# First-layer projections as seven half-size products, before and behind the dilated attention

## The chip, the cores and the metric

The kernel runs on one core of one Trainium2 chip. The metric is the device time of one execution in microseconds (us), as the median of several runs.

## What is computed

The reference is a network of two blocks in float32. Only the front of the first block matters here. An input of 1024 tokens by 1024 features is multiplied by one weight matrix, whose columns give the operands of a dilated attention (8 heads of 64), of a gated scan (4 heads), two rank-16 gate inputs and an output gate:

```
proj = jnp.einsum('bsd,df->bsf', h, w_in).astype(jnp.float32)
qa, ka, va, qb, kb, vb, lr_f, lr_b, gate = _split(
    proj, (A_WIDTH, A_WIDTH, A_WIDTH, B_K_WIDTH, B_K_WIDTH, B_V_WIDTH, B_GATE_RANK, B_GATE_RANK, MIX_WIDTH))
oa = dilated_attention(heads(qa, A_HEADS), heads(ka, A_HEADS), heads(va, A_HEADS), rel_bias)
...
ob = bidirectional_gated_scan(qh, kh, heads(g_f, B_HEADS), kh, heads(g_b, B_HEADS), heads(vb, B_HEADS))
```

Widths: qa, ka, va 512 each, qb and kb 512 each, vb 1024, the two low-rank inputs 32 together. The second block needs a conditioning vector for each of two inputs, silu(c) times a matrix of 1024 by 6144; it does not depend on the first block.

## The kernel before

The program is a row of stages, each a block of its own with a barrier behind it. The tiles have 128 partitions. The input is turned once into `xT` (feature blocks by tokens; KB is 8 blocks of 128 features) and stays in SBUF. The stages that matter:

- **prologue** loads the input and the first two weight units, turns the input on PE into `xT`.
- **project** ("in0") makes qa, ka and va. A unit is 256 weight columns. For a CHANNEL unit (result is channels by tokens) the stationary operand is a weight block of 128x128 and the moving one 512 tokens of `xT`: 32 products of 512 columns (L227). For a TOKEN unit the stationary operand is a token tile of `xT` and the moving one 256 weight columns: 64 products of 256 columns (L233). A product (one matmul of the program) is two records in the trace, since float32 is passed twice. Weights are double-buffered, eight PSUM banks are drained by ACT and DVE in turns, and ACT issues the stores.
- **dilated_attention** ("att") has 96 slots: 4 pairs of heads times 24 slots (3 dilations of 8 query tiles). In slot g PE does turn(g) (the transposes of the probabilities, L1804), score(g+2) (L1793), values(g-1) (L1816), sometimes total(u) (L1824), and then a share of the projections for the next stage, `Background` (L391, L395): the low-rank columns, qb, kb and vb. DVE does bias(g) (L1854, L1858: scores plus bias table and the row maximum), three conditioning products weigh (L1866, L1868: weights `w_ada` times silu(c), summed into `acc`), and move_out(g-2) (L1874: the attention's result out of PSUM). ACT does exps(g) (L1899), move(g-1) (L1908) and the drain of the background's fills (L408). score(g+2) on PE waits for bias(g+1) on DVE. A slot is wide (256 keys) in the first two dilations and narrow (128 keys) in the third.
- A fill is one PSUM bank's worth of background work. Six fills run as a lead ahead of the first score; the rest is spread over the 96 slots by columns: the product that would be the n-th column of all goes to slot n*96/total. A fill that ends in slot e is drained in slot e+1, its store is issued at step e+2 of the SP loop. Three PSUM banks and three stage buffers go round.
- The conditioning weights come in 24 units of 1 MB in three buffers. Units 0 to 7 are weighed for both vectors (16 products, 5.3 slots), units 8 to 23 for one (8 products, 2.7 slots). The load of unit u+3 is issued once unit u has been weighed; total(u) sums over partitions on PE, and unit u+2 can't be begun before it.
- All loads and stores of the stage are issued by SP from one list, in program order: first weights, then (after POOL has set constants, `consts`) the inputs of the first two head pairs (load(0), load(1): 20 DMAs each), the conditioning weights, and then slot by slot. load(2) and load(3) are issued when the stage of the head pair two before is done.
- **low_rank_scan** ("gla") follows, with the output gate's projections behind it.

Of the kernel before, what the change touches and what calls it, by code (L numbers as in the profile page):

```python
# [51 lines left out]
def prologue(nc, tag, src, dst, rel_bias, buckets, vectors, vpad, c, c_ctx, sT, weights, wbuf):  # L52

    T = SEQ // P
    W = wbuf[0].shape[2]
    with ExitStack() as ctx:
# [18 lines left out]
        def _(sp):  # L75
            for t in range(T):
                sp.dma_start(raw[:, t, :], src[t * P:(t + 1) * P, :]).then_inc(raw_loaded[t], 16)
            for b in range(2):
                sp.dma_start(wbuf[b][:, :, :], weights.rearrange("(k p) n -> p k n", p=P)[:, :, b * W:(b + 1) * W]).then_inc(w_loaded, 16)
# [6 lines left out]
            sp.wait_ge(w_loaded, 32)  # L86
# [199 lines left out]
class Background:  # L286
# [113 lines left out]
    def move(self, act, g):  # L400

        for f, end in enumerate(self.ended_in):
            if end != g - 1:
                continue
            job, m = self.job_of(f), self.count(f) // KB * self.columns(f)
            act.wait_ge(self.filled, f + 1)
            wait(act, self.stored[f % self.stages], 16 * (f // self.stages))
            act.activation(self.stage[f % self.stages][0:job.rows, 0:m], self.ps[f % self.banks][0:job.rows, 0:m], ACT.Copy).then_inc(self.moved, 1)  # L408

# [1199 lines left out]
def dilated_attention(nc, tag, qT, kT, vpad, vectors, attn, jobs, sT, ada_w, ada):  # L1609
# [6 lines left out]
    LEAD = 6  # L1616
# [3 lines left out]
    with ExitStack() as ctx:  # L1620
# [9 lines left out]
        p_sb = sb("p_sb", [P, 2, 2, 256])  # L1630
# [11 lines left out]
        w_ada = sb("w_ada", [P, 3, KB, ADA_W])  # L1642
        acc, ones, row = sb("acc", [P, 2, 2, ADA_W]), sb("ones", [P, 1]), sb("row", [1, 2, 2, ADA_W])
        ps_a = pbank("ps_a")
        ada_loaded, ada_stored = [sem(f"ada_loaded{b}") for b in range(3)], [sem("ada_stored0"), sem("ada_stored1")]
        weighted, summed, row_moved = (sem(n) for n in ("weighted", "summed", "row_moved"))
        bg = Background(sb, sem, pbank, jobs, HEADS * ST, 3, 3, 3, lead=LEAD)
# [46 lines left out]
        def _(sp):  # L1694
# [31 lines left out]
            def load_ada(u):  # L1726
                wait(sp, weighted, u - 2)
                src = ada_w[:, u * ADA_W:(u + 1) * ADA_W].rearrange("(k p) n -> p k n", p=P)
                sp.dma_start(w_ada[:, u % 3, :, :], src).then_inc(ada_loaded[u % 3], 16)

            def store_ada(u):
                sp.wait_ge(row_moved, u + 1)
                n = rows_of(u)
                sp.dma_start(ada[0:n, u * ADA_W:(u + 1) * ADA_W].rearrange("(a r) c -> a r c", a=1), row[:, u % 2, 0:n, :]).then_inc(ada_stored[u % 2], 16)
# [10 lines left out]
            bg.begin(sp)  # L1745
# [3 lines left out]
            load_ada(0)  # L1749
            load_ada(1)  # L1750
            load_ada(2)
            for g in range(LEAD):
                bg.transfer(sp, g)
            for g in range(HEADS * ST):
                bg.transfer(sp, LEAD + g)
                if g + 1 in unit_due and unit_due[g + 1] + 3 < ADA_UNITS:
                    load_ada(unit_due[g + 1] + 3)
                if g - 3 in unit_due:
                    store_ada(unit_due[g - 3])
# [5 lines left out]
            for b in range(2):  # L1765
                sp.wait_ge(ada_stored[b], 8 * ADA_UNITS)
# [4 lines left out]
        def _(pool):  # L1771
            make_identity(pool, ident)
# [7 lines left out]
            pool.memset(ident[0:1, 0:1], 1.0).then_inc(consts, 1)  # L1780

        @block.tensor
        def _(pe):
# [13 lines left out]
            def turn(g):  # L1797
# [4 lines left out]
                for h in range(2):  # L1802
                    for c in range(wide(d) // P):
                        last = pe.transpose(ps_t[:, h * 256 + c * P:h * 256 + (c + 1) * P], p_sb[:, s % 2, h, c * P:(c + 1) * P], ident[:, :])  # L1804
# [21 lines left out]
            pe.wait_ge(consts, 1)  # L1826
            for g in range(LEAD):
                bg.multiply(pe, g)
            score(0)
# [13 lines left out]
        def _(dve):  # L1843
            def bias(g):
# [6 lines left out]
                wait(dve, p_done, g - 1)  # L1851
# [8 lines left out]
            def weigh(u, kb, r):  # L1860
                if kb == 0 and r == 0:
                    dve.wait_ge(ada_loaded[u % 3], 16 * (u // 3 + 1))
                    wait(dve, summed, u - 1)
                mine, w, s = acc[:, u % 2, r, :], w_ada[:, u % 3, kb, :], sT[:, kb, r:r + 1]
# [11 lines left out]
            dve.wait_ge(consts, 1)  # L1876
            for g in range(HEADS * ST):
# [7 lines left out]
                if g > 1:  # L1885
                    move_out(g - 2)
            move_out(HEADS * ST - 2)
# [3 lines left out]
        def _(act):  # L1891
            def exps(g):
# [3 lines left out]

                wait(act, p_turned, g - 1)
# [3057 lines left out]
```

## Time and profile before

| | us |
|---|---|
| median of three runs | 4059.78 |
| the three runs | 4050.93 to 4068.09 |
| profiled execution, its run time | 4055.85 |
| profiled execution, span of the trace | 4054.2 |
| mean granted TensorE clock, share of full speed | 0.927 |

The trace is of one execution, with times from its start. In it the prologue lasts to 25.7 us, the projections ("in0") from 25.7 to 192.9 us, the attention stage from 199.0 to 689.3 us; of these its 96 slots from 260.1 to 683 us. PE is TensorE's matmul, PEld its weight load (it overlaps PE), DVE VectorE, ACT ScalarE, POOL GpSimd, SP SyncE; "SPq" is SP issuing a DMA. In a timeline the first two columns are start and duration, and brackets hold the idle time before the group and what ended it.

### The profile page before, as it was taken

How to read it: one execution, taken by the hardware profiler on the slowest of the kernel's cores; microseconds unless marked ns; L12 is line 12 of the kernel's file. 1: busy time of each engine (PE TensorE's matmuls, PEld its weight loads, DVE VectorE, ACT ScalarE, POOL GpSimd, SP SyncE). 2: the span in 40 equal slices, each digit the busy share in tenths (PEclk: the TensorE clock that was granted, in tenths of full speed). 3: DMA queues.
4: the chain of work that ended last, by engine and by line, in shares of the span. 5: the costliest groups of instructions: out<-in, count | busy, mean ns of one | idle time of the engine just before them, and what ended most of it. 6: DMA issues, size and time to landing. Idle time of an engine off the chain costs nothing. (4 is left out here: it accounts for less than half of the span.)

```text
span 4054.2 us, 47003 instructions
## 1 busy us (share of the span) xinstructions
PE 3560.9 (88%) x16369; PEld 2321.4 (57%) x16369; DVE 1821.6 (45%) x4038; ACT 1081.7 (27%) x2206; POOL 1179.5 (29%) x948
## 2 busy tenths in 40 slices
PE   8989998999798999999987698998877776949996
PEld 4645676777344667567546347564556775524442
DVE  1025552443573456666665460323479476240011
ACT  1023333442342233332432450221213212101111
POOL 0000000343343455555564362001212444211110
PEclk9999998999899999999999896998987877969998
DMA  3264542231532111211212532123334722347996
GB/s 116 68 183 143 151 133 86 80 103 58 217 147 60 55 57 45 66 56 41 72 38 71 220 137 76 47 64 101 105 86 144 252 75 101 121 185 241 319 320 233
DMA packets 409824, 494.01 MB, mean 122 GB/s; under 512 B 70514, under 2 KB 314506, under 8 KB 409603
## 3 DMA queue, kind: packets, MB, share of 16 engines
q1 hardware_dynamic: 380983, 457.42, 34.0%
q0 software_dynamic: 4608, 16.78, 1.6%
q10 hardware_dynamic: 24012, 16.97, 1.3%
q8 instruction: 126, 2.06, 0.2%
q14 instruction: 95, 0.78, 0.1%
HBM read 362.32 MB, written 128.77 MB: 121 GB/s over the span
## 5 line engine op out<-in xcount | busy, mean ns | idle before, releaser
L821 POOL TENSOR_TENSOR hgrn_queries<-hgrn_qd,hgrn_pair_decay 128x640 f32<-128x640 f32 x192 | 279.4, 1475 | 290.5 <-PE hgrn_ps_a L936 255.6
L871 PE MATMUL hgrn_ps_w<-xT,hgrn_ring 128*128 128x512 f32 x432 | 195.8, 600 | 1.8 <-PEq L34 1.8
L395 PE MATMUL gla_bg_ps<-gla_bg_w,xT 128*128 128x256 f32 x768 | 186.6, 388 | 4.3 <-DMA gla_bg_w<-in_w_in_ab_dram 4.3
L1473 PE MATMUL end_ps_z<-end_w,end_yT 128*128 128x512 f32 x384 | 168.7, 600 | 1.8 <-DMA end_w<-in_w_out_ab_dram 1.1
L2577 PE MATMUL end_ps_z<-end_w,end_yT 128*128 128x512 f32 x384 | 168.4, 599 | 0.8 <-ACT end_yT L2505 0.8
L395 PEld LDWEIGHTS gla_bg_ps<-gla_bg_w,xT 128*128 128x128 f32 x768 | 145.1, 194 | 35.0 <-issue 10.6
L391 PE MATMUL att_bg_ps<-xT,att_bg_w 128*128 128x512 f32 (+1 forms) x288 | 136.6, 614 | 13.3 <-POOL att_ident L1780 13.3
L45 POOL MEMSET gla_ident<- 128x128 f32 x1 | 0.2, 204 | 483.3 <-POOLq L34 483.3
L871 PEld LDWEIGHTS hgrn_ps_w<-xT,hgrn_ring 128*128 128x128 f32 x432 | 81.7, 193 | 94.1 <-issue 93.9
L871 PE MATMUL hgrn_ps_w<-hgrn_xs,hgrn_wsum 128*128 128x512 f32 x288 | 129.8, 599 | 5.3 <-ACT hgrn_sig L1153 5.3
L1041 DVE TENSOR_TENSOR hgrn_k_end<-hgrn_kd,hgrn_end_decay 128x128 f32<-128x128 f32 x168 | 127.1, 796 | 9.2 <-issue 2.6
L876 PE MATMUL hgrn_ps_w<-hgrn_ring,xT 128*128 128x256 f32 x576 | 128.8, 380 | 0.0
L2933 PE MATMUL in_ps<-hT_cols,in_w 128*128 128x512 f32 x288 | 126.2, 593 | 0.0
L1473 PEld LDWEIGHTS end_ps_z<-end_w,end_yT 128*128 128x128 f32 x384 | 73.1, 192 | 92.5 <-issue 89.0
L2577 PEld LDWEIGHTS end_ps_z<-end_w,end_yT 128*128 128x128 f32 x384 | 73.3, 193 | 90.5 <-issue 89.3
L4793 PE MATMUL exp_ps_d<-expw_wd,exp_hidT 128*128 128x512 f32 x256 | 114.2, 599 | 11.0 <-ACT exp_hidT L4740 11.0
L395 PE MATMUL att_bg_ps<-att_bg_w,xT 128*128 128x256 f32 x512 | 123.4, 387 | 0.0
L1899 ACT ACTIVATE att_p_sb<-att_s_sb,att_shift 128x256 f32<-128x256 f32 (+1 forms) x192 | 88.8, 464 | 121.4 <-DVE att_shift L1858 121.3
L227 PE MATMUL in_ps<-xT,in_wbuf 128*128 128x512 f32 x256 | 111.9, 600 | 9.0 <-PEq L34 9.0
L876 PEld LDWEIGHTS hgrn_ps_w<-hgrn_ring,xT 128*128 128x128 f32 x576 | 108.2, 191 | 14.1 <-issue 0.5
L4775 PE MATMUL exp_ps_g<-expw_wg,exp_xT 128*128 128x512 f32 x256 | 115.2, 604 | 0.7 <-ACT exp_xT L4729 0.7
L1056 DVE COPY_PREDICATED hgrn_scores<-hgrn_mask,hgrn_ps_s 128x128 f32<-128x128 uint32 x192 | 48.9, 299 | 147.2 <-issue 147.2
(645 smaller groups left out, 7744.2 us busy)
## 6 DMA issues: line engine op xcount, KB each, us to landing
expw_wg<-in_exp_w_gate_dram SPq DMA_DIRECT2D x16, 2048.0 KB, 10.3
expw_wu<-in_exp_w_up_dram SPq DMA_DIRECT2D x16, 2048.0 KB, 16.3
expw_wd<-in_exp_w_down_dram SPq DMA_DIRECT2D x16, 2048.0 KB, 21.9
att_w_ada<-in_ada_w_dram SPq DMA_DIRECT2D x24, 1024.0 KB, 6.3
hgrn_ring<-in_w_in_c_dram SPq DMA_DIRECT2D x18, 1024.0 KB, 5.4
end_gt<-gate_l SPq DMA_DIRECT2D x16, 768.0 KB, 8.5
hgrn_ring<-in_w_in_c_dram SPq DMA_DIRECT2D x24, 512.0 KB, 5.5
hgrn_o<-hgrn_o_stage SPq DMA_DIRECT2D x192, 64.0 KB, 1.6
```

The lines of the kernel that those rows point to most:

```text
L227: last = pe.matmul(bank[0:job.rows, 0:job.span], w[:, k, b * job.rows:(b + 1) * job.rows], job.acts[:, k, s:s + job.span], start=(k == 0), ...
L391: last = pe.matmul(bank[0:job.rows, 0:job.span], w[:, k, b * job.rows:(b + 1) * job.rows], job.acts[:, k, s:s + job.span], start=(k == 0), ...
L395: last = pe.matmul(bank[0:job.rows, q * job.width:(q + 1) * job.width], job.acts[:, k, t * P:t * P + job.rows], w[:, k, 0:job.width], star ...
L821: pool.tensor_tensor(queries[:, d, s, :].rearrange("p (b a c) -> p b a c", b=POINTS, a=PC), q, f, ALU.mult).then_inc(queries_done, 1)
L871: last = pe.matmul(bank[:, :], a[:, k, :], x(k), start=(fresh and k == 0), stop=(k == HK - 1), skip_group_check=True)
L876: last = pe.matmul(bank[:, q * 2 * P:(q + 1) * 2 * P], x(k)[:, t * P:(t + 1) * P], a[:, k, :], start=(fresh and q == 0 and k == 0), stop=( ...
L1041: dve.tensor_tensor(k_end[:, d, p % 2, :].rearrange("p (a c) -> p a c", c=CH), kd[:, b, d, t * P:(t + 1) * P].rearrange("p (a c) -> p a c" ...
L1473: made = pe.matmul(ps_z[h][:, :], yT[:, k, :], w[:, k, h * BANK:(h + 1) * BANK], start=(k == 0), stop=(k == NB - 1))
L2577: made = pe.matmul(ps_z[h][:, :], yT[:, k, :], w[:, k, halves[h]], start=(k == 0), stop=(k == NB - 1))
L2933: last = pe.matmul(ps[(3 * n + part) % 2][:, 0:span], w[u % 3][:, k, b * P:(b + 1) * P], acts, start=(k == 0), stop=(k == KB - 1))
L4775: last = pe.matmul(ps_g[:, :], xT[:, b, k, :], wg[:, b, k, :], start=(k == 0), stop=(k == KB - 1))
L4793: last = pe.matmul(ps_d[g][:, :], hidT[:, j, :], wd[:, b, j, g * BANK:(g + 1) * BANK], start=(j == 0), stop=(j == FB - 1))
```

## The change

Every projection of the first layer up to vb is computed in Strassen's form (Winograd's variant): the input `xT` and each weight unit of 256 columns are cut in two halves in both of their dimensions, and seven products of half the depth and half the width take the place of eight. Four sums of the input are made once (class `Halves` takes them as `xs`, and one quarter of `xT` is changed in place and restored at the start of low_rank_scan); four sums of each weight unit are made on POOL (`sums`, into `wsum` and into the unit itself). The seven products of a unit are seven fills: three of them are snapshots that ACT copies from PSUM to a stage buffer (`move`), three are added to such a snapshot by DVE on the way out (`join`), and the last is copied by ACT. A CHANNEL fill is 4 products of 512 columns, a TOKEN fill 16 products of 128 columns.

- `project` gives way to `project_halves`: first the low-rank columns (16 products of 512 columns, before in the attention's lead), then 6 units (qa, ka, va), one fill per step, SP issuing the stores. It ends by loading the first two units of the attention's background.
- In the attention, `Background` gives way to `Halves` with 8 units (56 fills) and 12 leading fills in place of 6 (34 fills before). PE no longer waits for `consts` before the lead, but before the first score. POOL makes the first unit's sums ahead of the constants. DVE joins at the end of its slot, behind move_out.
- Three stage buffers have fixed roles in place of going round: the fill LAST of unit u is moved into the buffer from which fill JOIN22 of the same unit has been stored.
- The conditioning weights have two buffers in place of three (load(u+2) when u has been weighed) and the row one in place of two; the probabilities are written over the scores, and bias(g) waits for turn(g-2) in place of exps(g-2).
- The prologue also loads the low-rank columns (128 KB).

The core of the diff:

```diff
-            dilated_attention(nc, "att", qa, ka, vpad, vectors, attn, [
-                Job(CHANNEL, xT, SEQ, w, 5 * A + B, 2 * RANK, 1, low),
-                Job(CHANNEL, xT, SEQ, w, 3 * A, 256, 2, qb),
-                Job(CHANNEL, xT, SEQ, w, 4 * A, 256, 2, kb),
-                Job(TOKEN, xT, SEQ, w, 5 * A, 256, 4, vb),
-            ], sT, ada_w_2[0], ada)
+            first = channels(0, qa) + channels(A, ka) + tokens(2 * A, vpad[VPAD:VPAD + SEQ, :], A)
+            second = channels(3 * A, qb) + channels(4 * A, kb) + tokens(5 * A, vb, B)
...
+                    project_halves(nc, "in0", xT, xs, ring, wsum, stage, first, second[0:2], low_w, low)
+                dilated_attention(nc, "att", qa, ka, vpad, vectors, attn, xT, xs, ring, wsum, stage, second, sT, ada_w_2[0], ada)
```

The roles of the seven fills, their banks and stage places, and what moves and joins wait for:

```diff
+    ROLE = {SNAP1: 0, PLAIN: 1, SNAP21: 0, SNAP22: 2, JOIN22: 0, JOIN21: 2, LAST: 0}
+    PLACE = {SNAP1: 0, PLAIN: 0, LAST: 2, SNAP21: 1, JOIN21: 1, SNAP22: 2, JOIN22: 2}
...
+    def move(self, act, g):
...
+            act.wait_ge(self.filled, f + 1)
+            wait(act, self.stored[place], 16 * {SNAP22: 2 * u, LAST: 2 * u + 1}.get(i, u))
+            act.activation(self.stage[:, place, :], self.ps[self.bank_of[f]][:, :], ACT.Copy).then_inc(self.moved, 1)
+
+    def join(self, dve, g):
...
+            dve.wait_ge(self.filled, f + 1)
+            dve.wait_ge(self.moved, self.nth[snap])
+            dve.tensor_tensor(into, self.ps[self.bank_of[f]][:, :], into, ALU.add).then_inc(self.added, 1)
...
+    def multiply(self, pe, g, x_made=None):
...
+                e = self.before_on[f]
+                if e is not None:
+                    pe.wait_ge(self.added if self.fills[e][1] in self.BY_DVE else self.moved, self.nth[e])
```

`before_on[f]` is the fill that used the same bank before. With three banks in the attention, bank (u + role) mod 3, fill SNAP21 of a unit waits for SNAP1 of that unit to be moved.

```diff
             def load_ada(u):
-                wait(sp, weighted, u - 2)
+                wait(sp, weighted, u - 1)
...
-            bg.begin(sp)
+            bg.load(sp, 2)
+            load_ada(0)
             sp.wait_ge(consts, 1)
             load(0)
             load(1)
-            load_ada(0)
             load_ada(1)
-            load_ada(2)
             for g in range(LEAD):
                 bg.transfer(sp, g)
             for g in range(HEADS * ST):
                 bg.transfer(sp, LEAD + g)
-                if g + 1 in unit_due and unit_due[g + 1] + 3 < ADA_UNITS:
-                    load_ada(unit_due[g + 1] + 3)
+                if g + 1 in unit_due and unit_due[g + 1] + 2 < ADA_UNITS:
+                    load_ada(unit_due[g + 1] + 2)
...
-                wait(dve, p_done, g - 1)
+                wait(dve, p_turned, g - 1)
...
                 if g > 1:
                     move_out(g - 2)
+                bg.join(dve, LEAD + g)
...
+            low_rows = slice(0, KB // 2)
+            dve.tensor_tensor(xT[:, low_rows, BANK:SEQ], xT[:, low_rows, BANK:SEQ], xT[:, low_rows, 0:BANK], ALU.add).then_inc(restored, 1)
```

Three places show the moved instructions. The first is SP's queue at the start of the attention stage, before the change: the loads of the second head pair end (the last `att_tab`), three conditioning loads follow, and then the first stores of the lead's fills.

```order
L1711 DMA att_tab<-vectors 128x128
L1729 DMA att_w_ada<-in_ada_w_dram 128x8x256 x3
L347 DMA low<-att_bg_stage 32x512
L336 DMA att_bg_w<-in_w_in_ab_dram 128x8x256
L347 DMA low<-att_bg_stage 32x512
L347 DMA qb<-att_bg_stage 128x512 x3
```

The same place after it.

```order
L1956 DMA att_tab<-vectors 128x128
L1974 DMA att_w_ada<-in_ada_w_dram 128x8x256
L508 DMA qb<-l_stage 128x512 x3
L489 DMA l_ring<-in_w_in_ab_dram 128x8x256
L508 DMA qb<-l_stage 128x512 x4
L489 DMA l_ring<-in_w_in_ab_dram 128x8x256
```

The first stores of fills still stand behind all loads of two head pairs; one conditioning load went ahead of them and one is gone.

The second place is DVE in a slot of the attention, before: after move_out comes the next slot's bias.

```order
L1874 COPY att_stage<-att_ps_o 128x128
L1854 ISA att_s_sb,att_stage<-att_ps_s,att_tab 128x256
L1854 ISA att_stage 128x1
L1854 ISA att_s_sb,att_stage<-att_ps_s,att_tab 128x256
L1854 ISA att_stage 128x1
L1858 TENSOR_SCALAR att_shift<-att_stage 128x2
```

After, in a slot that follows the end of a joined fill.

```order
L2120 COPY att_stage<-att_ps_o 128x128
L588 TENSOR_TENSOR l_stage<-att_bg_ps,l_stage 128x512
L2100 ISA att_s_sb,att_stage<-att_ps_s,att_tab 128x256
L2100 ISA att_stage 128x1
L2100 ISA att_s_sb,att_stage<-att_ps_s,att_tab 128x256
L2100 ISA att_stage 128x1
L2104 TENSOR_SCALAR att_shift<-att_stage 128x2
```

The join came between move_out and the next bias; there are 20 of them behind the slots and 4 in the lead.

The third place is SP's queue behind the load of the fourth head pair (load(3)), before.

```order
L1711 DMA att_tab<-vectors 128x192 x4
L1711 DMA att_tab<-vectors 128x128
L1729 DMA att_w_ada<-in_ada_w_dram 128x8x256
L1734 DMA ada<-att_row 1x256
L351 DMA vb<-att_bg_stage 128x2x256
L1729 DMA att_w_ada<-in_ada_w_dram 128x8x256
```

After.

```order
L1956 DMA att_tab<-vectors 128x192 x4
L1956 DMA att_tab<-vectors 128x128
L489 DMA l_ring<-in_w_in_ab_dram 128x8x256
L1974 DMA att_w_ada<-in_ada_w_dram 128x8x256
L1979 DMA ada<-att_row 1x256
L508 DMA vb<-l_stage 128x4x128
L1974 DMA att_w_ada<-in_ada_w_dram 128x8x256
```

The first conditioning load behind load(3) was that of unit 13 and is now that of unit 12, and a weight load of 1 MB stands ahead of it.

## Rows read from the trace of the kernel before

**Rows 1.** Busy time by stretch, inside the attention: PE, PEld, DVE, ACT, POOL, clock, DMA.

```profile
300.00:350.00 50.00, 50.00 (x215) 28.72 (x215) 25.26 (x100) 18.37 (x60) 0.00 (x0) 1.00 0.33 101
```

**Rows 2.** The first projections' two product lines, and their first sixteen records.

```profile
L227 PE MATMUL in_ps<-xT,in_wbuf x256: 592/592/1192, 25.7 to 137.0; 128*128 128x512 f32 x128
...
L233 PE MATMUL in_ps<-in_wbuf,xT x256: 378/379/380, 137.4 to 192.5; 128*128 128x256 f32 x128
...
25.68 8.90 PE L227 MATMUL in_ps<-xT,in_wbuf 128*128 128x512 f32 x16 [9.04 <-PEq L34]
```

**Rows 3.** PE in order of time, products of 128 columns in the second layer.

```profile
1402.85 0.39 PE L933 MATMUL hgrn_ps_a<-hgrn_v_in,hgrn_scores 128*128 128x128 f32 x2
...
1403.74 7.07 PE L876 MATMUL hgrn_ps_w<-hgrn_ring,xT 128*128 128x256 f32 x32
```

**Rows 4.** SP's queue in order of time, from the attention stage's start.

```profile
199.02 1.65 SPq L336 DMA_DIRECT2D att_bg_w<-in_w_in_ab_dram  x3
206.12 0.34 SPq L1698 DMA_DIRECT2D att_q<-qa  x1
...
239.32 5.88 SPq L1729 DMA_DIRECT2D att_w_ada<-in_ada_w_dram  x3
245.25 2.83 SPq L347 DMA_DIRECT2D low<-att_bg_stage  x1
```

**Rows 5.** ACT behind the lead; landing of the load issued at 239.3.

```profile
254.15 0.60 ACT L408 ACTIVATE att_bg_stage<-att_bg_ps 128x512 f32<-128x512 f32 x1 [24.38 <-DMA low<-att_bg_stage]
...
257.66 1.28 ACT L1899 ACT_TABLE_LOAD   x1
...
DMA to landing us min/median/max: 8.6/8.6/8.6
```

**Rows 6.** PE at the attention stage's start, in order of time.

```profile
206.15 43.58 PE L391 MATMUL att_bg_ps<-xT,att_bg_w 128*32 128x512 f32 x96 [13.31 <-POOL att_ident L1780]
249.66 0.70 PE L1793 MATMUL att_ps_s<-att_k,att_q 64*128 64x256 f32 x4
...
260.10 1.12 PE L1804 MATMUL att_ps_t<-att_ident,att_p_sb 128*128 128x128 f32 x4 [7.75 <-ACT att_p_sb L1899]
```

**Rows 7.** All engines around one slot of the attention.

```profile
325.07 1.94 PE L391 MATMUL att_bg_ps<-xT,att_bg_w 128*128 128x512 f32 x4
325.27 0.29 DVE L1874 COPY att_stage<-att_ps_o 128x128 f32<-128x128 f32 x1 [3.65 <-PE att_ps_o L1816]
325.48 0.41 DVE L1854 CUSTOM_DVE_ANT_0 att_s_sb<-att_ps_s,att_tab 128x256 f32<-128x256 f32 x1
...
326.32 0.17 DVE L1858 TENSOR_SCALAR att_shift<-att_stage 128x2 f32<-128x2 f32 x1
...
326.84 0.60 PE L1804 MATMUL att_ps_t<-att_ident,att_p_sb 128*128 128x128 f32 x4
...
327.37 0.84 PE L1793 MATMUL att_ps_s<-att_k,att_q 64*128 64x128 f32 x4
```

**Rows 8.** Second layer: a join on DVE, a weight sum on POOL, DVE beside POOL.

```profile
L970 DVE TENSOR_TENSOR hgrn_gstage<-hgrn_ps_w,hgrn_gstage x20: 677/692/693, 1315.3 to 1928.7; 128x512 f32<-128x512 f32 x20
...
L762 POOL TENSOR_TENSOR hgrn_wsum<-hgrn_ring x24: 1261/1272/2437, 1240.8 to 2113.3; 128x512 f32<-128x512 f32 x18, 128x1024 f32<-128x1024 f32 x6
...
L1041 DVE TENSOR_TENSOR hgrn_k_end<-hgrn_kd,hgrn_end_decay x168: 277/750/2439, 1367.8 to 2202.0; 128x128 f32<-128x128 f32 x168
```

**Rows 9.** SP around the fourth head pair's load; landing of the load at 494.27.

```profile
474.94 0.62 SPq L1724 DMA_DIRECT2D attn<-att_stage  x1
...
492.89 0.43 SPq L1729 DMA_DIRECT2D att_w_ada<-in_ada_w_dram  x1
...
DMA to landing us min/median/max: 11.9/11.9/11.9
```

**Rows 10.** DVE begins conditioning unit 12.

```profile
492.50 0.35 DVE L1866 TENSOR_SCALAR att_acc<-att_w_ada,sT 128x256 f32<-128x256 f32 x1 [3.12 <-PE att_ps_a L1824]
```

**Rows 11.** Who waited for whom in the slots: total, times, longest.

```profile
DVE att_acc L1866 <- PE att_ps_a L1824: 46.1, 15, 4.3
```

More of the change, by code:

```diff
@@ L1771, in _ @@
         def _(pool):
+            bg.sums(pool, 0)
             make_identity(pool, ident)
@@ L1780, in _ @@
             pool.memset(ident[0:1, 0:1], 1.0).then_inc(consts, 1)
+            for u in range(1, len(units)):
+                bg.sums(pool, u)
         @block.tensor
@@ L1876, in _ @@
             dve.wait_ge(consts, 1)
+            for g in range(LEAD):
+                bg.join(dve, g)
             for g in range(HEADS * ST):
@@ L4831, in network @@
             w = w_in_ab[0]
-            with ExitStack() as first_weights:
-                wbuf = [first_weights.enter_context(nc.sbuf_tensor(f"in0_wbuf{b}", [P, KB, 256], F32)) for b in range(2)]
-                prologue(nc, "pro", x[0], xT, rel_bias, buckets, vectors, vpad, c_2, c_ctx_2, sT, w, wbuf)
-                project(nc, "in0", [
-                    Job(CHANNEL, xT, SEQ, w, 0, 256, 2, qa),
-                    Job(CHANNEL, xT, SEQ, w, A, 256, 2, ka),
-                    Job(TOKEN, xT, SEQ, w, 2 * A, 256, 2, vpad[VPAD:VPAD + SEQ, :]),
-                ], loaded=wbuf)
@@ L4840, in network @@
[L4840 to L4847 removed]
+            low_at = 5 * A + B
@@ new lines, in network @@
+            channels = lambda col, dst: [Unit(CHANNEL, w, col + UNIT_W * n, dst, UNIT_W * n) for n in range(A // UNIT_W)]
+            tokens = lambda col, dst, width: [Unit(TOKEN, w, col + UNIT_W * n, dst, UNIT_W * n) for n in range(width // UNIT_W)]
+            first = channels(0, qa) + channels(A, ka) + tokens(2 * A, vpad[VPAD:VPAD + SEQ, :], A)
+            second = channels(3 * A, qb) + channels(4 * A, kb) + tokens(5 * A, vb, B)
+            with ExitStack() as shared:
+                held = lambda n, *shape: shared.enter_context(nc.sbuf_tensor(n, [P, *shape], F32))
+                ring, wsum = held("l0_ring", 3, KB, UNIT_W), held("l0_wsum", 3, KB // 2, P)
+                stage, xs = held("l0_stage", 3, BANK), held("l0_xs", 3, KB // 2, BANK)
+                with nc.sbuf_tensor("l0_low_w", [P, KB, 2 * RANK], F32) as low_w:
+                    prologue(nc, "pro", x[0], xT, rel_bias, buckets, vectors, vpad, c_2, c_ctx_2, sT, w, ring, low_w, low_at)
+                    project_halves(nc, "in0", xT, xs, ring, wsum, stage, first, second[0:2], low_w, low)
+                dilated_attention(nc, "att", qa, ka, vpad, vectors, attn, xT, xs, ring, wsum, stage, second, sT, ada_w_2[0], ada)
@@ L4848, in network @@
+            low_rank_scan(nc, "gla", 4, B // 4, qb, kb, vb, low, gla_gate_up[0], gla_gate_bias[0], gla_o, 1 / 16, scale, xT, [
+                Job(TOKEN, xT, SEQ, w, low_at + 2 * RANK, 256, 6, gate_l0),
             ])
```

246 lines of the change are left out of this document (217 added, 29 removed).

## The prediction

> **What bounds the kernel now.** I read the stretches first, then each engine's timeline over three places. Inside the attention PE is busy for the whole 50 us at the full clock (1.00), while DVE has 25 us of work and ACT 18 [rows 1]. So in the slots each product taken off PE shortens the time, as long as DVE, ACT and SP keep up. Two places differ. At the stage's start SP spends 206.1 to 239.3 us issuing the loads of two head pairs, and only at 245.25 comes the first store of a fill [rows 4]; ACT stands until 254.15 on that store, and PE, which finished the lead at 249.7, can turn only at 260.1 [rows 5, 6]. The second is SP around load(3): 18 us from 474.9 to 492.9 pass before a conditioning load gets through [rows 9].
>
> **Price of a product.** 128 products of 512 columns run from 25.68 to 137.4; the first sixteen records take 8.9 us, the other 120 products 103 us, 0.858 each. The start at the half clock (1.2 GHz) costs 1.9 us more. 128 products of 256 columns take from 137.4 to 192.7, 0.432 each [rows 2]. The nearest thing to the new TOKEN products is four pairs of records of 128 columns, each with its own weight load, between 1402.85 and 1403.74: 0.111 a record, 0.223 a product [rows 3]. A CHANNEL unit so falls from 32 to 28 products of 0.858 (27.5 to 24.0 us), a TOKEN unit from 64 x 0.432 = 27.6 to 112 x 0.223 = 25.0 us.
>
> The Trainium skill, "TensorE: Matmul & The Clock Gate", section "Back-to-back issue gap", speaks against this step: in a stream of weight loads and products it gives about 81 ns a matmul at 128 columns where the isolated gap is 56. No run here shows that ratio; the row above stands at the bare column rate.
>
> **The change, part by part** (against the profiled execution, 4055.85 us; it lies 3.9 us under the median and inside the spread of the three runs).
>
> *Projections ahead of the attention.* Four CHANNEL units give 16 x 0.858 = 13.7 us, two TOKEN units 55.3 - 50.0 = 5.3, and the low-rank products (16, one pass of 512 columns each) come in from the lead: +13.7. Sum -5.3. The four input sums on DVE and the first weight sums on POOL lie beside those low-rank products. Later weight sums: three of 1.27 us and the gaps between them (4.3 us, rows 8) must be ready two fills (6.9 us) after the last unit's end: hidden, for as long as POOL does nothing else. The prologue's extra 128 KB in small lines: 0 to 2 us, I take +0.7. The last store is 256 KB in place of 1 MB, so the barrier comes sooner: 0 to -2, I take -1.
>
> *The lead.* Call the attention stage's start T (199.0). Before, the first turn is at T + 61.1 [rows 4, 6]. PE may now start at T, not at T + 7.1. But the stage buffers decide. POOL makes four sums first (4 x 1.43 = 5.7 us), so `consts` comes at T + 12.8, and load(0) and load(1) take 33.2 us of SP: T + 46.0. Only then, behind one conditioning load, come the stores. That load lands 8.6 us after its issue [rows 5], the two stores PLAIN and JOIN22 of unit 0 (0.5 MB) some 1.4 us later by the 2.8 us per MB at which the two further loads pushed the low-rank store back [rows 4, 5]: T + 56.0. LAST of unit 0 is moved into JOIN22's place, so ACT stands until then; behind it stands the move of SNAP1 of unit 1, and PE's tenth fill waits for that. PE has done nine fills (36 x 0.858 + 1.9 = 32.8 us), idles some 24 us, resumes at T + 57.4 at the half clock, does 12 products (10.3 + 1.9) and scores at T + 69.6. Bias and score take 1.9 us, table load, exponentials and turn 2.4 (257.66 to 260.10, rows 5, 6): turn at T + 74. Cost: **+13 us**. Bounds: 0 if small stores pass the load ahead of them and PE resumes 13 us sooner, +18 if SP is held at each store as before (2.8 us).
>
> *The slots: less PE work.* Before 96 products of 512 columns and 256 of 256, now 64 and 448 of 128: -27.5 - 10.7 = **-38.2 us**, 0.4 a slot.
>
> *The slots: joins on DVE.* The join sits behind move_out and ahead of the bias for which score waits. Before: values' issue ends at 325.07, DVE copies at 325.27, bias is done at 326.49, PE reaches score at 327.37, 0.53 after turn: 0.9 us of slack [rows 7]. After a joined fill ends (F), DVE starts 0.2 later, holds 0.60 for the join (0.69 long, rows 8, started on by 0.09), 1.01 for bias, 0.05 to PE: F + 1.86. PE wants it at the end of the slot's products plus 0.53. The stall is 1.33 less what PE still multiplies in that slot behind F. By the plan's rule, of 19 joined fills that end in slots seven end with the slot (9.3 us), three have one product of 512 columns behind them (0.47 each, 1.4), and nine TOKEN ones have two (three fills, 0.88), three (0.66), four (two fills, 0.44), five (0.22) or six (none): 4.4. Sum **+15 us**; bounds 5 (wait times partly absorbed) and 19 x 1.33 = 25. ACT's drains were there before, and its exponentials have a whole slot of slack.
>
> *The slots: conditioning in two buffers.* At one-row units a load has about three slots. It lands in 5 to 12 us [rows 5, 9]; while SP is free that is enough. Not at load(3): SP is held from 474.9 to 492.9, then issues 1 MB of weights and only then unit 12's load, which is thus the second megabyte, and the second one before (494.27) landed 11.9 us on, at 506 [rows 9]. DVE reached unit 12 at 492.5 [rows 10]; in slots 0.4 us shorter that is 491. It waits 14.5 us with the bias queued behind, PE stands with it, and restarts at the half clock: **+16.5 us**; bounds 6 and 20. Load(2) falls among two-row units with twice the time: 0.
>
> *Smaller terms.* DVE already waits 46 us in 15 units for total(u-2) [rows 11]; with 0.4 us less of products behind it PE feels more of that: 0 to 6, I take +3. POOL's 24 sums in the slots run beside DVE, and an instruction of DVE beside POOL had a median of 0.75 us where its least was 0.28 [rows 8]; this meets the weighs rather than the bias: 0 to 10, +3. The Trainium skill, "SBUF — State Buffer", section "SBUF: two separate sides", has the rule: a DVE instruction with two SBUF inputs and a GpSimd one exclude each other for the whole instruction. By it no weigh waits over 1.27 us, and bias and join, which read one operand from PSUM, don't wait. The shorter idle before the first turn saves a half-clock start: -1. Writing the probabilities over the scores costs nothing: turn(g-2) stands ahead of score(g) on PE, which bias(g) waits for anyway. Restoring `xT` is one DVE instruction of four times a join's columns, at a stage start where DVE has nothing: 0, at most 2.8.
>
> **Sum:** -5.3 + 0.7 - 1 + 13 - 38.2 + 15.1 + 16.5 + 3 + 3 - 1 = +5.8; 4055.85 + 5.8 = 4061.7, so **4062 us**. PE loses 43.5 us of work and gets it back as waiting.
>
> **Rivals.**
> 1. *The waits are mostly absorbed (faster).* PE's queue and DVE's idle half [rows 1] swallow them: lead +5 (small stores pass), joins +8, unit 12's load +6. That is 8 + 7 + 10.5 = 25.5 less: 4036. For it: DVE was idle 3.65 us ahead of the copy in rows 7. Against: what counts is the order behind it, and the idle time lies ahead of the copy. Chance 0.22.
> 2. *Two conditioning buffers are late at every one-row unit (slower).* Decisive is whether issue delay plus landing exceeds three slots, 12 us. A store that waits for a joined fill can hold SP most of a slot (4 us); with 5 to 7 us of landing it is short of 12, behind another megabyte it is over. If 13 more units are late by 2 us: +26, 4088. Chance 0.14.
> 3. *128-column products are held by their weight loads (slower).* At 1.45 times 0.223, 672 products cost 0.10 each more: +67, 4129. The ratio of the two figures of the skill's page on TensorE, above, is 1.45. For it: weight loads of 0.19 us each lie behind one another. Against: rows 3. Chance 0.06.
> 4. *The change doesn't do what it says:* fills blocked in banks and places throughout, beyond the lead. The roles leave two fills between a store and its reuse, about 7 us against a landing of 3: 0.03, some 4100.
>
> **How the numbers follow.** The forecast has 0.55; its terms' bounds (lead -13/+5, joins -10/+10, unit 12 -10/+4, small ones -6/+10) give 4040 to 4082. With rival 1 below and rival 2 above, 8 in 10 lie in **4034 to 4090**. Half a percent (20 us) is about what measuring this kernel can tell from no change. Faster by more (under 4039.5): rival 1 with most of its chance and the forecast's lower edge, 0.24. Slower by more (over 4080): rivals 2 to 4 and the upper edge, 0.20. Within: 0.56.
>
> **What would show it.** PE idle of some 24 us within the lead, ended by ACT's move of SNAP1, itself ended by a store of `qb`; the first turn 74 us behind the stage's start. A DVE wait of 10 to 15 us at the first `att_acc` of unit 12, ended by a DMA, and no like wait elsewhere. PE waits on `att_shift` of 0 to 1.3 us, some 19 of them with a join in front. Products of 128 columns 0.111 apart a record: were they 0.16, rival 3 holds. "in0" 5 us shorter. Wrong it would be if the first turn came by T + 62, or if the slots took under 405 us (423 before, 422 by my terms).

## The result, and the profile after

| | kernel before | changed kernel |
|---|---|---|
| median of the runs | 4057.65 us (4050.93 to 4068.09, 9 runs) | 4071.05 us (4066.08 to 4080.92, 9 runs) |
| ratio to before | 1 | 1.0034, interval 1.0023 to 1.0045 |
| profiled execution: own time | 4055.85 us | 4071.05 us |
| first projections ("in0"), first to last product | 167.2 us | 162.3 us |
| attention stage's start, T | 199.0 | 192.75 |
| first turn | T + 61.1 | T + 71.7 |
| first turn to last values | 423.1 us | 431.8 us |

The forecast was 4062 us with a range of 4034 to 4090, and no change as the likeliest case: 0.56. The time came inside the range, 9 us above the forecast and 0.34% above the kernel before.

PE in order of time over the start of the attention stage and at its end (start, length, what it does, in brackets the idle time before it and what ended it):

```profile
185.06 3.74 PE L562 MATMUL in_ps<-l_wsum,xT 128*128 128x128 f32 x32
192.79 9.62 PE L560 MATMUL att_bg_ps<-xT,l_ring 128*128 128x512 f32 x16 [4.00 <-PEq L34]
...
249.40 8.65 PE L560 MATMUL att_bg_ps<-l_xs,l_wsum 128*128 128x512 f32 x16 [22.95 <-ACT l_stage L576]
257.88 3.60 PE L560 MATMUL att_bg_ps<-xT,l_ring 128*128 128x512 f32 x8
261.40 0.70 PE L2039 MATMUL att_ps_s<-att_k,att_q 64*128 64x256 f32 x4
...
264.49 0.66 PE L2050 MATMUL att_ps_t<-att_ident,att_s_sb 128*128 128x128 f32 x4 [0.42 <-ACT att_s_sb L2147]
...
695.76 0.56 PE L2062 MATMUL att_ps_o<-att_v,att_pT 128*128 128x64 f32 x4
```

These rows answer to [rows 6]. PE starts the lead at the stage's first moment, does nine fills, stands 22.95 us and turns at 264.49. What it stood for is in ACT's and SP's timelines, answering to [rows 5] and [rows 4]:

```profile
248.26 1.08 ACT L576 ACTIVATE l_stage<-att_bg_ps 128x512 f32<-128x512 f32 x2 [38.34 <-DMA qb<-l_stage]
...
258.69 1.28 ACT L2147 ACT_TABLE_LOAD   x1
```

```profile
205.35 0.34 SPq L1943 DMA_DIRECT2D att_q<-qa  x1
...
219.15 1.17 SPq L1943 DMA_DIRECT2D att_q<-qa  x1
...
237.12 0.43 SPq L1974 DMA_DIRECT2D att_w_ada<-in_ada_w_dram  x1
237.61 3.95 SPq L508 DMA_DIRECT2D qb<-l_stage  x3
```

SP issues load(0) and load(1) from 205.35 to 237.1, then a conditioning load of 1 MB, and only then the stores of `l_stage`, one of which ACT needs: 38.34 us of standing on ACT, 22.95 of them felt by PE.

The second place is unit 12. SP's queue (answering to [rows 9]), then DVE (to [rows 10]) and PE:

```profile
474.24 0.66 SPq L1943 DMA_DIRECT2D att_q<-qa  x1
...
490.88 1.03 SPq L489 DMA_DIRECT2D l_ring<-in_w_in_ab_dram  x1
491.96 0.72 SPq L1974 DMA_DIRECT2D att_w_ada<-in_ada_w_dram  x1
```

```profile
503.12 0.35 DVE L2112 TENSOR_SCALAR att_acc<-att_w_ada,sT 128x256 f32<-128x256 f32 x1 [13.81 <-DMA att_w_ada<-in_ada_w_dram]
```

```profile
505.21 1.23 PE L2039 MATMUL att_ps_s<-att_k,att_q 64*128 64x256 f32 x4 [11.97 <-DVE att_shift L2104]
```

The waits over the whole stage, 190 to 700 us (engine, what it waited for; us in total, times, longest):

```profile
PE att_ps_s L2039 <- DVE att_shift L2104: 36.0, 28, 12.0
...
PE att_bg_ps L560 <- ACT l_stage L576: 22.9, 1, 22.9
...
DVE att_acc L2112 <- DMA att_w_ada<-in_ada_w_dram: 13.8, 1, 13.8
```

In the slots alone (264 to 697) the first row is 34.7 us in 27 waits; in the kernel before the same row, 262 to 683, is 0.8 us in two. Less the 12.0 of unit 12, that leaves 22.7 us in 26 short waits.

A third place lies behind the slots, at the start of low_rank_scan. PE's first product there waits for POOL to make `gla_ident`; the first row is from the kernel before, the others from the changed one:

```profile
693.78 0.69 PE L2142 MATMUL gla_ps_s<-gla_ident 128*128 128x128 f32 x2 [10.60 <-POOL gla_ident L2050]
...
702.80 2.29 DVE L2516 TENSOR_TENSOR xT<-xT 128x2048 f32<-128x2048 f32 x1 [6.15 <-PEq L34]
703.16 2.08 POOL L47 TENSOR_SCALAR_AFFINE_SELECT gla_ident<-gla_ident 128x128 f32<-128x128 f32 x1 [0.20 <-issue]
708.83 0.69 PE L2390 MATMUL gla_ps_s<-gla_ident 128*128 128x128 f32 x2 [12.51 <-POOL gla_ident L2298]
```

POOL's instruction, 0.29 us in the kernel before, takes 2.08 and ends 0.15 us behind DVE's restoring of `xT` (702.80 to 705.09). PE waits 12.51 us in place of 10.60.

What the prediction had far too small is in the stretches (busy time of the engines, then PE's granted clock, DMA share, GB/s), which answer to [rows 1]:

```profile
300.00:350.00 50.00, 47.35 (x207) 27.08 (x206) 26.66 (x98) 18.16 (x59) 0.00 (x0) 0.97 0.26 81
340.00:350.00 10.00, 8.77 (x30) 4.12 (x29) 5.28 (x21) 2.89 (x11) 0.00 (x0) 0.83 0.28 83
500.00:550.00 50.00, 42.21 (x264) 33.16 (x265) 24.82 (x85) 17.22 (x52) 0.00 (x0) 0.88 0.34 106
```

and the same at 500 in the kernel before:

```profile
500.00:550.00 50.00, 50.00 (x271) 37.86 (x269) 24.56 (x90) 18.46 (x57) 0.00 (x0) 1.00 0.50 162
```

Stretches of 10 us from 270 to 680 all have clock 1.00 in the kernel before. In the changed kernel twelve of those up to 690 have less: 0.83 to 0.86 at 340, 420, 550 and 570, 0.91, 0.50 and 0.91 from 490 to 520, and five between 0.90 and 0.99. Length times (1 - clock), added up, is 15.3 us. About 3.5 us of it falls where PE stood for unit 12 (493.2 to 505.2), which costs nothing twice; **12 us** is left: 3.3 behind unit 12's wait, and five dips of 1.7 us each (at 340, 410 to 430, 540 to 560, 570 to 590, 650 to 670). Most short waits have no dip behind them: 26 waits stand beside five dips, and two waits of 1.27 us (ending at 370.0 and 471.7) were followed by none. What decides it isn't shown by any run here. How such a dip looks in PE's own rows:

```profile
341.36 0.38 PE L2050 MATMUL att_ps_t<-att_ident,att_s_sb 128*128 128x128 f32 x2
342.97 0.84 PE L2039 MATMUL att_ps_s<-att_k,att_q 64*128 64x128 f32 x4 [1.23 <-DVE att_shift L2104]
343.75 0.66 PE L2062 MATMUL att_ps_o<-att_v,att_pT 128*128 128x64 f32 x4
344.33 1.60 PE L2070 MATMUL att_ps_a<-att_acc,att_ones 128*1 128x512 f32 x2
345.87 2.07 PE L560 MATMUL att_bg_ps<-xT,l_wsum 128*128 128x512 f32 x2
347.74 0.54 PE L2050 MATMUL att_ps_t<-att_ident,att_s_sb 128*128 128x128 f32 x2
...
349.47 1.94 PE L560 MATMUL att_bg_ps<-xT,l_wsum 128*128 128x512 f32 x4
```

After a wait of 1.23 us, two records of 512 columns take 1.60 and two more 2.07; four take 1.94 a slot later. In stretches of 1 us the granted clock is 0.82 from 344 to 345, 0.50 from 345 to 348 and 0.98 from 348 to 349: the half clock (1.2 GHz) comes some 1.7 us behind the wait's end, and the full one (2.4 GHz) is back some 5 us behind it.

### The profile page after: what moved, and what is told of

It reads as the page before. It is cut to its first block and busy times, and to the rows that moved or that the text cites. A ratio compares the mean times of both kernels' runs of the same rounds, so it can differ in the third digit from the quotient of the medians.

```text
span 4069.3 us, 48185 instructions
## 1 busy us (share of the span) xinstructions
PE 3533.5 (87%) x16881; PEld 2323.9 (57%) x16881; DVE 1866.2 (46%) x4073; ACT 1087.5 (27%) x2218; POOL 1252.8 (31%) x1004
## 5 line engine op out<-in xcount | busy, mean ns | idle before, releaser
L530 POOL TENSOR_TENSOR l_wsum<-l_ring 128x512 f32<-128x512 f32 x14 | 20.0, 1432 | 548.9 <-PE att_bg_ps L562 202.4
L2147 ACT ACTIVATE att_s_sb<-att_s_sb,att_shift 128x256 f32<-128x256 f32 (+1 forms) x192 | 88.9, 464 | 169.9 <-DVE att_shift L2104 169.8
L2114 DVE SCALAR_TENSOR_TENSOR att_acc<-att_w_ada,sT,att_acc 128x256 f32<-128x256 f32 x224 | 118.7, 543 | 14.2 <-issue 0.9
L2039 PE MATMUL att_ps_s<-att_k,att_q 64*128 64x256 f32 (+1 forms) x384 | 91.5, 559 | 36.1 <-DVE att_shift L2104 36.0
L2321 POOL TENSOR_TENSOR gla_queries<-gla_qd,gla_pair_decay 128x640 f32<-128x640 f32 x64 | 87.2, 1382 | 84.5 <-PE gla_ps_o L2384 61.0
```

The costliest lines, as they stand in the source:

```text
L2114: last = dve.scalar_tensor_tensor(out=mine, in0=w, scalar=s, in1=mine, op0=ALU.mult, op1=ALU.add)
```

## Experiments on the four waits

Where did 43 us of saved PE work go? My theory: into three separate waits (the lead, the joins, unit 12), each with lost clock behind it. The rival: they are one limit, DVE or SP, which shows up elsewhere once one of them is removed. Five kernels change one thing each. All ran against the same kernel before, whose median was 4056.87 to 4057.65 us in every group of runs; the ratios have intervals of 0.1 to 0.2% (4 to 6 us) either way, so two gains that lie closer than that can't be ranked.

**Head-pair loads in pieces.** SP no longer issues a load of 20 DMAs at once, but two a slot:

```
-                    load(j + 2)
+                if j and s < 10 and j + 1 < HEADS:
+                    load(j + 1, slice(2 * s, 2 * s + 2))
```

> The changed kernel, but the 20 DMAs of load(2) and of load(3) are issued two per slot over ten slots (24 to 33, 48 to 57) in place of in one piece. My theory: unit 12 of the conditioning is late only because SP is held 17 us by load(3). So DVE's 13.8 us wait at unit 12 falls to under 3 us, PE's 12.0 us wait at score goes with it, and so does the stretch at the half clock behind it (499 to 512 us in the changed kernel's trace, some 5 us lost): 12 + 5 = 17 us less, 4054. Rival (the load is late because two buffers are too few at one-row units, whoever holds SP): the wait moves to other one-row units, less than 5 us gained, over 4066.

Measured: 4052.57 us, 0.9991 of before (0.9982 to 1.0001), so 18.5 us less than the changed kernel. The longest wait of PE at score is 1.9 us, and DVE has no wait for `att_w_ada` any more. Unit 12's late load was SP's doing. In the changed kernel's own rows it costs 15.3 us, 12.0 of waiting and 3.3 of half clock behind it, where 16.5 had been put down; that the run gave 18.5, with load(2) spread as well, lies within the intervals.

**The lead's stores ahead of load(1).**

```
             load(0)
-            load(1)
...
                 bg.transfer(sp, LEAD + g)
+                if g < 10:
+                    load(1, slice(2 * g, 2 * g + 2))
```

> The changed kernel, but load(1) is no longer issued ahead of the lead's stores: its 20 DMAs go two per slot over slots 0 to 9. My theory: PE's 22.9 us wait in the lead is ACT's wait for the store of fill JOIN22, which stands behind load(1) and load(0) on SP. Without load(1) SP is free 17 us sooner, at 22 us behind consts' 12.6, and the store lands at about T + 36, when PE has just done its ninth fill (T + 33): the wait falls to 0 to 4 us, score comes at about T + 48 in place of T + 68.7, 20 us less, 4051. Rival (SP is only late, not the cause; the next loads in the slots are pushed back in turn): the first slots wait for stores and conditioning loads instead, less than 8 us gained, over 4063.

Measured: 4057.43 us, 0.9995 (0.9985 to 1.0005), 13.6 less. PE's wait in the lead fell, but not to the 0 to 4 us that I had expected:

```profile
PE att_bg_ps L560 <- ACT l_stage L576: 7.9, 1, 7.9
```

and the first turn came 15.4 us sooner. The slots then took 1.1 us more, with unit 12's wait at 13.6 and more half clock around it (0.52 and 0.63 in the 10 us stretches at 480 and 490). The remaining 7.9 us are, for the most part, the stores' landing behind the 1 MB conditioning load, which is still issued ahead of them: the last version below takes that load away too, and the wait falls to 1.0.

**The join behind the next slot's bias.** DVE still does every join, one slot later:

```
                 bias(g)
+                if g:
+                    bg.join(dve, LEAD + g - 1)
...
-                bg.join(dve, LEAD + g)
```

> The changed kernel, but DVE joins a fill one slot later and behind bias, not ahead of it; the joins and their number stay. My theory: 27 waits of PE at score in the slots, 22 us without the long one, come mostly from joins that stand ahead of the bias; with the half-clock stretches that follow some of them (344, 419, 549, 574 to 584, 659 us: 8 us lost by the granted clock) they cost 20 to 30. Expected: 15 to 22 us less, 4052, and PE's waits at score under 8 us beside unit 12's. Rival (the waits come from POOL's sums that stretch DVE's weighs, or from the total-before-weigh wait, which stay): under 6 us gained, over 4065.

Measured: 4051.49 us, 0.9985 (0.9976 to 0.9995), 19.6 less. PE's waits at score, 190 to 690:

```profile
PE att_ps_s L2039 <- DVE att_shift L2104: 23.5, 15, 12.4
```

The short waits, without unit 12's, fell from 24.0 to 11.1 us, 12.9 less (I had expected under 8 to be left). Most of the other 6.7 was clock: the stretches from 330 to 430 lose 1.7 us here and 3.4 in the changed kernel, those from 520 to 670 none, and 5.1 in the changed kernel; around unit 12 (480 to 520) it lost 1.8 more than there.

**Small joins.** Is it the join's work or its place?

```
-                bg.join(dve, LEAD + g)
+                bg.join(dve, LEAD + g, 8)
```

> The changed kernel, with each join in the attention's slots over 8 of its 512 columns (the rest of the sum is left out, so the projections made in the slots are incomplete); order, waits and stores are as before. It separates the join's 0.69 us of DVE work from its place: DVE standing on the fill's end with the bias queued behind. Theory: the place weighs as much as the work. By the prediction's own terms a stall of 1.33 us less what PE has behind the fill becomes one of 0.73: seven fills that end with the slot keep 0.73 (5.1 us) and the others about 1 in all, so 15 falls to 6, plus some clock: 9 to 13 us less, 4060. Rival: only the work counts; then taking it away is worth what moving it behind the bias was, 19.6: 4051.5.

Measured: 4058.94 us, 1.0000 (0.9989 to 1.0011): 12.1 less, by the first theory. Short waits are 16.8 us:

```profile
PE att_ps_s L2039 <- DVE att_shift L2104: 29.9, 23, 13.1
```

The same joins done in full behind the bias give more (19.6) than joins with hardly any work in their old place. The difference fits DVE standing on the fill's end with the bias queued behind; the two runs' intervals just overlap, so the order of the two is likely and not certain.

**Small weight sums on POOL.**

```
             for u in range(1, len(units)):
-                bg.sums(pool, u)
+                bg.sums(pool, u, few=True)
```

> The changed kernel, but POOL makes the weight sums of units 1 to 7 of the attention over 8 of 128 columns only; the rest of the sums is left out. Takes away POOL's 1.27 us instructions beside DVE and nothing else. My theory: each set of sums stretches one slot's weighs (three weighs of 1.44 us took 4.46 at 483 us), PE feels 0.5 to 1.5 us of it, six times: 3 to 9 us less, 4065. Rival (they are the main cause of the waits at score): 15 us less or more, under 4057.

Measured: 4063.89 us, 1.0014 (1.0005 to 1.0024), 7.2 less, short waits 18.8 us where the changed kernel has 24.0. Its trace is of an execution of 4072.82 us, 8.9 above that median, so the 5.2 us less of waits can't be set against the 7.2 one to one. In the changed kernel the trace shows how it comes about. POOL's four sums of one unit, and DVE beside them:

```profile
481.76 1.27 POOL L530 TENSOR_TENSOR l_wsum<-l_ring 128x512 f32<-128x512 f32 x1 [59.90 <-PE att_bg_ps L562]
...
486.05 1.27 POOL L536 TENSOR_TENSOR l_wsum<-l_ring,l_wsum 128x512 f32<-128x512 f32 x1 [0.16 <-issue]
```

```profile
482.42 0.63 DVE L2104 TENSOR_SCALAR att_shift<-att_stage 128x2 f32<-128x2 f32 x1
483.14 4.46 DVE L2114 SCALAR_TENSOR_TENSOR att_acc<-att_w_ada,sT,att_acc 128x256 f32<-128x256 f32 x3
...
505.25 1.60 DVE L2114 SCALAR_TENSOR_TENSOR att_acc<-att_w_ada,sT,att_acc 128x256 f32<-128x256 f32 x3
```

```profile
488.79 0.70 PE L2039 MATMUL att_ps_s<-att_k,att_q 64*128 64x256 f32 x4 [1.46 <-DVE att_shift L2104]
```

Three weighs took 4.46 us beside POOL and 1.60 without it, so about 0.95 more each; bias and PE behind them were late by 1.46. The Trainium skill's rule on the shared port ("SBUF — State Buffer", "SBUF: two separate sides"), cited in the prediction, agrees for the weighs: each was held back by no more than one sum's 1.27. That bias doesn't wait, which the prediction drew from the rule, holds in this trace for its two reductions (0.41 us each, as always) and not for its last instruction, which reads SBUF alone: L2104 took 0.63 us at 482.42 until the first sum ended, where its median is 0.17, and up to 1.26 elsewhere in the slots.

## Is it the waits that bring the clock down?

The changed kernel has two new things in its slots: waits of about a microsecond, and 448 projection products of 128 columns, each with a weight load of its own. Either could lie behind the dips. The kernel before has neither, and no dip. (The attention's own turns and narrow scores have 128 columns in both kernels, so "no 128-column products" in the expectations holds for the projections only.) So I gave it the waits alone, by doing DVE's two bias reductions, and the drain behind them, three times in 24 of 96 slots; in the first kernel every fourth, in the second in four groups of six:

```
-                for h in range(2):
+                for h in (0, 1, 0, 1, 0, 1) if 2 < g % 4 else range(2):
```

```
+                for h in (0, 1, 0, 1, 0, 1) if 11 < g % 24 < 18 else range(2):
```

> The kernel before (no 128-column products in its slots, no clock loss in them either), with DVE's two bias reductions done three times in every fourth slot (24 of 96), so that PE waits at score for DVE there. Four more reductions of 0.4 us are 1.6 us, less the 0.9 us of slack of rows 7: 0.7 us of PE wait in 24 slots, 17 us. Theory: the chip answers clusters of such short waits with a lower granted clock, so the slots lose 5 to 12 us more to the clock where they lost none: 4057 + 17 + 8 = 4082. Rival: the clock loss of the changed kernel comes from its 128-column products with their many weight loads, not from waits; then the granted clock in these slots stays 1.00 and the time is 4057 + 17 = 4074.

> As the kernel whose bias reductions are done three times in 24 slots of the kernel before, but with those slots in four groups of six on end (12 to 17 of every 24). The PE waits are the same 17 us. Theory: if it is waits that bring the clock down, then waits close together do it more surely than waits apart: the groups show a granted clock of 0.5 to 0.9 and lose 5 to 15 us more, 4057 + 17 + 10 = 4084, with the clock at 1.00 in the slots between the groups. Rival (128-column products are the cause): clock 1.00 throughout the slots, 4074.

Measured: 4078.67 us, 1.0053 (1.0037 to 1.0068), and 4074.64 us, 1.0045 (1.0029 to 1.0060): 21.2 and 17.2 us above the kernel before. PE's waits at score, slots apart and slots together:

```profile
PE att_ps_s L1793 <- DVE att_shift L1859: 13.0, 19, 0.9
```

```profile
PE att_ps_s L1793 <- DVE att_shift L1859: 10.2, 13, 1.2
```

and one stretch of each in which the clock fell:

```profile
330.00:340.00 10.00, 9.12 (x36) 5.57 (x37) 5.35 (x25) 3.57 (x13) 0.00 (x0) 0.83 0.73 234
```

```profile
420.00:430.00 10.00, 9.11 (x35) 4.87 (x34) 7.59 (x34) 2.48 (x8) 0.00 (x0) 0.83 0.01 3
```

| | waits more than before | clock lost, 270 to 680, before: 0 | sum | measured |
|---|---|---|---|---|
| waits apart | 12.2 | 6.8 | 19.0 | 21.2 |
| waits together | 9.4 | 8.5 | 17.9 | 17.2 |

The times alone would not decide, since the waits came out shorter than the 17 us I had put down. The clock does: it fell in five and in six stretches (four and five dips of 1.7 us) of slots whose projections have no product of 128 columns. Short waits are enough; over all of them, each microsecond of waiting lost another 0.6 to 0.9 to the clock. These are averages over a few dips in one execution each, and no price of a single wait: again most waits have no dip behind them. DVE's extra work by itself isn't the cause: in the first of the two stretches shown DVE was busy for 5.35 of 10 us, and the kernel before has 6.73 (600 to 610 us) at a clock of 1.00. The part of my expectation on groups held as to place (the dips at 310, 420 to 450 and 540 to 570 lie at three of the four groups), while the total over the groups is hardly above that of the waits apart. In the changed kernel 22.7 us of short waits stand beside 12 us of lost clock, 3.3 of it unit 12's restart; the other 8.5 are 0.4 a microsecond. That 128-column products add nothing isn't shown by itself, but there is no sign of it: the three edits together (below) have them all, and lose 5 us in their slots for 11.1 of waits, 0.5 a microsecond.

## A version faster than both

**The three edits together.** Loads in pieces, the lead's stores first, joins behind the bias; the diff is the sum of the three above.

> The changed kernel with all three edits of the first experiments at once: head-pair loads issued two pieces a slot, load(1) behind the lead's stores, and the join moved behind the next slot's bias. My theory: three separate waits, at three places, and each slot or lead wait also costs granted clock. Singly they gave 18.5, 13.6 and 19.6 us against the changed kernel's 4071; at separate places they add up: 4071 - 51.7 = 4019, 0.9% under the kernel before, with under 15 us of PE waits left at score and under 6 us of clock loss in the slots. Rival: each removed wait moves the limit to DVE or SP, which are then late elsewhere: less than two thirds of the sum arrives, over 4036.

Measured: 4021.14 us (4018.21 to 4025.46), 0.9914 of before (0.9900 to 0.9927), 49.9 less than the changed kernel where 51.7 was the sum of the single gains. They are three limits, not one. The stage's waits, 190 to 690:

```profile
PE att_ps_s L2046 <- DVE att_shift L2111: 11.1, 14, 1.9
PE att_bg_ps L560 <- ACT l_stage L576: 5.6, 1, 5.6
```

**The second conditioning load out of the lead too.**

```
             load(0)
-            load_ada(1)
...
                 bg.transfer(sp, LEAD + g)
+                if g == 0:
+                    load_ada(1)
```

> The kernel with the three edits together, and the second conditioning load (1 MB) taken out of the lead too: issued in slot 0, behind the lead's stores. With the three edits ACT still stood 21 us on the stores behind that megabyte, and PE 5.58 us. Theory: the stores land some 3 us sooner (2.8 us per MB, the price of the prediction), PE's wait falls to 0 to 3 us and the half clock behind it goes: 3 to 6 us less, 4016. Rival: unit 1 of the conditioning is now late in the slots and gives it back as a DVE wait: 4021 or more.

Measured: 4014.53 us, 0.9895 (0.9879 to 0.9912), 6.6 less. PE's wait on `l_stage` is down from 5.6 to 1.0 us, as expected:

```profile
PE att_bg_ps L560 <- ACT l_stage L576: 1.0, 1, 1.0
```

This is the fastest version, 1.05% under the kernel before. Its median rests on four runs that reach from 4013.96 to 4023.47 (the profiled one), and its interval overlaps that of the three edits, so the step from the kernel with three edits is likely and not certain.

**Is the gain in the lead one of the old kernel's too?** The kernel before with load(1) in pieces over slots 0 to 9, and nothing else:

> The kernel before, with only load(1) of the attention taken out of the lead and issued in pieces over slots 0 to 9. It prices SP's hold at the stage start in the old kernel: PE waited 7.75 us for the low-rank store and then stood at half clock. Theory: that wait goes except for the store's own landing, and the half-clock restart shrinks: 5 to 9 us less, 4050. Rival: the store waits for the 1 MB conditioning load as before (it is issued behind it), nothing moves: 4057.

Measured: 4047.01 us, 0.9974 (0.9963 to 0.9985), 10.4 less than before, 1.4 more than the upper end I gave. The 7.75 us in front of the first turn [rows 6] is gone from its trace. Against this kernel, the fastest version is 32.5 us faster, of the 43.5 us of PE work that the prediction counted. No run shows what the seven products alone are worth. The change also lets PE begin the lead with the stage, where the old kernel's PE stands 7.1 us for POOL's constants, and the fastest version still has 11.1 us of waits at score.

## Why the prediction came out as it did

| term | predicted | measured |
|---|---|---|
| in0 | -5.3 | -4.9 |
| start and handover | -0.3 | -1.4 |
| lead, T to first turn | +13 | +10.6 |
| slots, PE work | -38.2 | -37.2, by difference: what is left of the slots' +8.7 |
| joins | +15.1 | 12.9 of waits, the run with the join moved |
| total(u-2), POOL beside DVE | +6 | 9.8 of waits, the rest of 22.7; 5.2 of it POOL's sums |
| unit 12's load | +16.5, with 2 of clock | 12.0 of waits |
| clock in the slots, from 270 us on | -1 (and the 2 above) | +12 |
| rest of the program | 0 | +2.1 |

*Right.* The structure: PE's work fell, and most of it came back as waiting at the places named. That it fell by what was counted is measured for "in0" (4.9 of 5.3); in the slots the 37.2 is what closes the sum, and so only fits the 38.2. (The measured terms add up to 15.9 less the 0.8 of waits that were there before; the two profiled executions lie 15.2 apart.) The lead's stall was 22.95 (24 predicted), PE resumed at T + 56.7 (T + 57.4), `consts` came at T + 12.6 (T + 12.8), unit 12's wait was 13.81 (14.5) and ended by the DMA named. Token products of 128 columns ran at the price of [rows 3], so the rival of weight-bound products fell:

```profile
163.62 7.31 PE L562 MATMUL in_ps<-l_ring,xT 128*128 128x128 f32 x64
170.76 7.31 PE L562 MATMUL in_ps<-l_wsum,l_xs 128*128 128x128 f32 x64
```

That is 0.112 a record from start to start, where [rows 3] had 0.111 and the rival wanted 0.16. The ratio that the Trainium skill gives for such a stream ("TensorE: Matmul & The Clock Gate", "Back-to-back issue gap"), about 81 to 56 ns, does not show in this trace. The short waits together came to 22.7 us where joins, totals and POOL had been given 21. The two parts were less well placed than their sum: joins 2 us too high, the others 4 too low.

*Mis-sized.* One term carries the miss: the clock, "-1" among the smaller terms and the 2 us within unit 12's 16.5. I let the half clock follow long stops only, as [rows 2] and [rows 6] show it, and took [rows 1], with its 1.00, as the state of the slots in general. But PE had hardly any waits there (two of 0.4 us in all the slots), so the trace of before could not show what waits of 0.7 to 1.5 us do. The runs that put such waits into the kernel before did: 0.6 to 0.9 us of lost clock for each microsecond of them. Of the 12 us, 8.5 are dips behind short waits, for which the sum had nothing, and 3.3 the restart behind unit 12, for which it had 2. With +12 in place of +1 the slots come to +8.7 and not to -1.6. That is 10.3 us of a miss of 9.3; the rest (lead -2.4, start and handover -1.1, in0 +0.4, and +2.1 behind the slots) all but cancels, and that is luck.

The +2.1 is a term that the prediction put at 0: restoring `xT`, "at a stage start where DVE has nothing". DVE has nothing there, but POOL makes `gla_ident` in the same two microseconds, and its instruction of 0.29 us took 2.08 beside DVE's 2.29. PE, which waits for it, began 1.9 us later behind the last values than in the kernel before. It's the same in every trace: POOL's instruction took 2.08 us in all eight kernels that restore `xT` and 0.29 in all four that don't, and PE's wait there was 12.1 to 13.0 against 10.3 to 10.6. No run moved the restoring alone.

*The rivals.* "Two buffers late at every one-row unit" didn't occur: DVE waited once for `att_w_ada`. "Waits absorbed" didn't either: 22.7 us of short waits were felt. Nor were fills blocked throughout: PE waited once for `l_stage`, in the lead. Both signs that would have spoken against the forecast stayed away: the first turn came at T + 71.7 and not by T + 62, and the slots took 431.8 us and not under 405.

## What to carry to other kernels

When a change takes work off the engine that bounds a stage, look in the same breath at what its waits will do to its clock: short stops spread over a stage, which a trace with none cannot price, cost 1.4 to 1.9 times their length here. A queue that is issued in program order (SP) makes each block of many DMAs a wall for everything behind it; spread over slots, the same loads gave back 18.5 and, in the lead, 13.6 us. An instruction that waits for an engine's latest result belongs behind the one that this engine needs next, not ahead of it: that move was worth more than taking nearly all of the instruction's work away.

## What I had not expected of the hardware

The granted clock of PE fell to 1.2 GHz in a stage in which PE was about 95% busy. In the stretch 300 to 350 of the changed kernel PE was busy 47.35 of 50 us and had 0.97; from 344.6, some 1.7 us behind a wait of 1.23, its products ran at half rate, and at 349.47 at full rate again. In the kernel before, with DVE's work lengthened in 24 slots and all else as it was, 19 waits of at most 0.9 us left five stretches of 10 us at 0.83 to 0.97, where every stretch from 270 to 680 had 1.00.
